# A hybrid Fourier/pooling encoder block on one core: xn is transposed by VectorE in squares of 32 instead of by TensorE, and the sums of the seven products of `w_out` are begun in PSUM from copies that ScalarE puts into the banks

## The reference, cut to what matters

```python
h = rmsnorm(x, norm1_g)
z = h @ w_in
ya = fourier_mix(z[..., :512]) ; yb = pool_mix(z[..., 512:])
x = x + concatenate([ya, yb]) @ w_out          # the stage of this change
h = rmsnorm(x, norm2_g)                        # its result is stored transposed
x = x + (silu(h @ w_gate) * (h @ w_up)) @ w_down
return rmsnorm(x, normf_g)
```

## Time and profile before

| | before |
|---|---|
| time, median of 3 runs (lowest to highest) | 2491.96 us (2491.36 to 2492.42) |
| profiled execution: its time, its span | 2491.23 us, 2489.4 us |
| TensorE, VectorE, ScalarE busy | 99%, 67%, 39% of the span |
| granted clock of TensorE | 1.00 in every stretch |
| pairs 2 to 11 of the output projection | 384 to 593 us, 20.86 us for each |

### The profile page before, as it was taken

The page is one execution under the profiler, slowest core; times in us unless marked ns, Lnnn a source line. Parts: engine busy times, 40 slices in busy tenths (PEclk is TensorE's granted clock), DMA queues, the critical chain, the costliest instruction groups (busy, mean ns, idle before and its releaser), DMA issues.

```text
span 2489.4 us, 32156 instructions
## 1 busy us (share of the span) xinstructions
PE 2474.7 (99%) x11141; PEld 2049.1 (82%) x11141; DVE 1676.6 (67%) x2600; ACT 965.2 (39%) x1830; POOL 166.9 (7%) x222
## 2 busy tenths in 40 slices
PE   9999999999999999999999999999999999999998
PEld 7888878887888888888888888888888888888887
DVE  5555788779767767877677687666774564455565
ACT  5534566667333333433333343333332232233333
POOL 2555400000000000000000000000000000000000
PEclk9999999999999999999999999999999999999999
DMA  6433767666423222532232432232346654354554
GB/s 184 115 85 99 223 221 254 238 238 260 157 80 116 97 103 110 195 113 110 80 126 101 155 146 96 110 110 89 118 186 217 242 200 168 119 196 149 195 189 148
DMA packets 154373, 381.99 MB, mean 153 GB/s; under 512 B 11992, under 2 KB 48184, under 8 KB 145076
## 3 DMA queue, kind: packets, MB, share of 16 engines
q1 hardware_dynamic: 145616, 350.81, 40.8%
q0 software_dynamic: 8240, 29.94, 3.2%
q10 hardware_dynamic: 432, 0.14, 0.0%
HBM read 254.22 MB, written 126.62 MB: 153 GB/s over the span
## 4 chain that ended last, share of the span: by engine, by line
PE 85%; DVE 2%; ACT 1%; issue 0%; DMA 0%; DVEq 0%
PE bank L351 28%; PE bank L353 28%; PE bank L352 28%; PE bank L2020 1%; ACT a_hi L2401 0%; DVE a_lo L2592 0%; DMA a_raw<-ha_scr 0%; PE bank L1373 0%; PE bank L1059 0%; DVE x L1818 0%; ACT h_out L1637 0%; DVE scratch L1033 0%; DVE zy_late L1044 0%; DVE uv_lo L1071 0%; ACT xn L1627 0%
## 5 line engine op out<-in xcount | busy, mean ns | idle before, releaser
L351 PE MATMUL bank<-a_hi,w_hi 128*128 128x512 f32 x1848 | 719.4, 389 | 2.0 <-DVE w_lo L2603 1.6
L352 PE MATMUL bank<-a_lo,w_hi 128*128 128x512 f32 x1848 | 718.9, 389 | 0.0
L353 PE MATMUL bank<-a_hi,w_lo 128*128 128x512 f32 x1848 | 718.9, 389 | 0.0
L351 PEld LDWEIGHTS bank<-a_hi,w_hi 128*128 128x128 f32 x1848 | 346.9, 188 | 75.6 <-DVE w_lo L2603 2.8
L353 PEld LDWEIGHTS bank<-a_hi,w_lo 128*128 128x128 f32 x1848 | 347.0, 188 | 72.0
L352 PEld LDWEIGHTS bank<-a_lo,w_hi 128*128 128x128 f32 x1848 | 347.0, 188 | 71.7
L351 PE MATMUL bank<-t_hi,s_hi 128*128 128x512 f32 x924 | 359.4, 389 | 0.0
L352 PE MATMUL bank<-t_lo,s_hi 128*128 128x512 f32 x924 | 359.4, 389 | 0.0
L353 PE MATMUL bank<-t_hi,s_lo 128*128 128x512 f32 x924 | 359.4, 389 | 0.0
L2414 ACT ACTIVATE w_hi<-t_raw 128x512 fp32r<-128x512 f32 x256 | 162.3, 634 | 462.4 <-PE bank L353 378.8
L2753 DVE TENSOR_TENSOR s_lo<-s_raw,s_hi 128x512 fp32r<-128x512 f32 x231 | 156.2, 687 | 230.7 <-ACT s_hi L2489 230.7
(11 more groups left out here) (277 smaller groups left out, 3163.1 us busy)
## 6 DMA issues: line engine op xcount, KB each, us to landing
s_scr<-sums_out SPq DMA_DIRECT2D x33, 1792.0 KB, 5.9
s_raw<-s_scr SPq DMA_DIRECT2D x42, 1024.0 KB, 5.0
w_raw<-in_w_gate SPq DMA_DIRECT2D x64, 512.0 KB, 3.5
w_raw<-in_w_up SPq DMA_DIRECT2D x64, 512.0 KB, 4.3
wd_staged<-in_w_down SPq DMA_DIRECT2D x121, 256.0 KB
a_raw<-ha_scr SPq DMA_DIRECT2D x21, 1024.0 KB, 5.0
s_raw<-s_scr SPq DMA_DIRECT2D x21, 768.0 KB, 4.4
x<-in_x SPq DMA_DIRECT2D x24, 512.0 KB, 4.9
```

The costliest lines, as they stand in the source:

```text
L351: pe.matmul(out, w_hi, m_hi, start=first, stop=False, **checks)
L352: pe.matmul(out, w_hi, m_lo, start=False, stop=False, **checks)
L353: return pe.matmul(out, w_lo, m_hi, start=False, stop=last, **checks)
```

## The change

On TensorE, the transposes go for 20 of the 24 tiles (tiles 0, 1, 22 and 23 keep them). VectorE turns xn in squares of 32x32 in their stead, four instructions of 128x512 for a pair (`turn_squares`). A square-wise transpose leaves the features spread differently over partitions, so that the gain is now a value of each partition and square: ScalarE multiplies `h_out` in place in 32 instructions of 2x32 columns for a pair (`gains`), where `stage_h` had 16 of 128. The rows reach their places in DRAM through the stores: `store_squares` has 8 + 4 stores of 32 partitions in packets of 512 bytes, 3584 of them for a pair. The token order inside a block changes, and the feed-forward matmuls read it back by a moving operand of 16 runs of 32 columns (`tokens_of`), where it was 4 runs of 128.

The sums of the seven products change too. ScalarE copies the first product (bank 0) into bank 1, TensorE adds the third product on top of it, ScalarE copies that sum into bank 3, and TensorE adds the fifth and the seventh on it. `u_sums` with its five VectorE additions becomes two (`add_held`). The two norms of a pair are one (`variance`, `inverse` over two columns), and so `scaled` of both tiles stands behind it. `combine` moves to the end of VectorE's pair.

```diff
-        def u_sums(n, k, par):
-            ...
+        def add_held(n, k, par, i):
+            tile, c, bank = ((1, 1, 2), (0, 1, 1))[i]
...
+            dve.tensor_tensor(at, o_ps[bank][:, :], at, ALU.add).then_inc(u_summed, 1)
...
+        def turn_squares(n, a, tile):
+            if (a, tile) == (0, 0):
+                dve.wait_ge(halves_out, halves_stored(n - 1))
+            if a == 0:
+                dve.wait_ge(xn_ready, n * 2 + (tile + 1))
+            half = xn[:, tile, a * HALF:(a + 1) * HALF].rearrange("p (k m f) -> p m k f", m=ROWS, f=SQUARE)
+            done = dve.transpose(h_out[:, tile, 4 * a:4 * a + 4, :].rearrange("p m (k t) -> p m k t", t=SQUARE), half)
...
+        def gains(n, a, first, last):
+            act.wait_ge(transposed, turned(n, a))
+            for b in range(first, last):
+                m, k = divmod(b, 4)
+                d = 4 * a + k
+                both = h_out[:, :, 4 * a + m, k * SQUARE:(k + 1) * SQUARE]
+                out = act.activation(both, both, ACT.Identity, scale=gain_squares[:, m, d:d + 1])
...
         def copy_product(n):
-            act.activation(U[:, :], o_ps[0][:, :], ACT.Copy).then_inc(p_copied, 1)
+            act.activation(o_ps[1][:, :], o_ps[0][:, :], ACT.Copy).then_inc(p_copied, 1)
+
+        def copy_sum(n):
+            act.wait_ge(pair_ready, product_of(n, 2))
+            act.activation(o_ps[3][:, :], o_ps[1][:, :], ACT.Copy).then_inc(p_copied, 1)
...
-        MORE = (False, False, False, True, False, True, True)
+        MORE = (False, False, True, True, True, True, True)
...
-            transposes(n * 2 - 2, slot)
             ready(S2, T2)
+            pe.wait_ge(p_copied, n * 2 - 3)
             seventh(S2)
-            transposes(n * 2 - 1, slot + 1)
...
+            pe.wait_ge(p_copied, n * 2 - 2)
             seventh(S3)
...
+        def store_squares(n):
+            sp.wait_ge(h_staged, staged(n))
+            for i in range(ROWS):
+                ... (2 stores of h_out rows i*32 to i*32+32)
+            sp.wait_ge(h_combined, n * 4 + 4)
+            for i in range(ROWS):
+                ... (1 store of h_sums)
...
+        def tokens_of(a, k):
+            return a[:, :, :].rearrange("p q (i k t) -> p (q i) k t", i=ROWS, t=SQUARE)[:, :, k, :]
```

More of the change, by code:

```diff
@@ L1559, in pair @@
             next_x(2 * n - 1, slot + 1, before + 1)
-            store_h(n - 1, 1 - par)
+            store_squares(n - 1)
         def load_a(s):
-            sp.dma_start(ahead.a_raw[s][:, :, :], ha_scr[A_ORDER[s], 0, :, :, :]).then_inc(ahead.a_loaded[s], DMA)
+            sp.dma_start(ahead.a_raw[s][:, :, :], ha_scr[0, A_ORDER[s], :, :, :]).then_inc(ahead.a_loaded[s], DMA)
         for n in range(2, LAST):
             if n == LAST - 1:
-                for par in range(2):
-                    sp.wait_ge(h_stored[par], 2 * 3 * DMA)
+                sp.wait_ge(halves_out, halves_stored(3))
+                sp.wait_ge(sums_out, sums_stored(3))
             pair(n)
@@ L1650, in scalar @@
         round_y(1)
-        act.wait_ge(ahead.gains_loaded, 2 * DMA)
+        act.wait_ge(ahead.gains_loaded, (2 + ROWS) * DMA)
         round_y(2)
@@ L1686, in pair @@
             round_v(after, k_after, 1 - par, A11)
-            scaled(n * 2 - 1, slot + 1)
-            stage_h(n * 2 - 2, slot, (h_stored[par], k * (3 * DMA)))
+            scaled(n, slot)
+            scaled(n, slot + 1)
             round_v(after, k_after, 1 - par, S1)
-            stage_h(n * 2 - 1, slot + 1)
-            for v in (S2, A12, S3):
-                round_v(after, k_after, 1 - par, v)
+            copy_sum(n)
+            gains(n - 1, 0, 0, 16)
+            round_v(after, k_after, 1 - par, S2)
+            gains(n - 1, 1, 0, 8)
+            round_v(after, k_after, 1 - par, A12)
+            gains(n - 1, 1, 8, 16)
+            round_v(after, k_after, 1 - par, S3)
             squares(n * 2, 2 * par, n * 4 + 3)
             round_v(after, k_after, 1 - par, S4)
-            root(n * 2, 2 * par)
         in_turn(act, pair)
-        round_v(LAST, NT // 4 - 1, 1, A22)
-        scaled(NT - 4, 0)
+        norms(LAST, NT // 4 - 1, 1)
+        scaled(LAST, 0)
+        scaled(LAST, 1)
         act.wait_ge(y_ready, split(LAST, A22))
         feed.round_a(0, 0)
[L1702 to L1707, removed]
+        copy_sum(LAST)
+        gains(LAST - 1, 0, 0, 16)
         feed.round_a(0, 1)
         feed.round_w(0, 0, 0, 0)
-        stage_h(NT - 3, 1)
+        gains(LAST - 1, 1, 0, 16)
         feed.round_w(0, 0, 0, 1)
@@ L1934, in vector @@
         rounds = NT // 4 - 1
-        c21(LAST - 1, 0)
-        for v in (A22, S3, S4):
-            rest_of_v(LAST, 1, v)
+        norms(LAST, 1)
         feed.rest_of_a(0, 0)
-        variance(NT - 3, 1)
-        inverse(NT - 3, 1)
-        u_sums(LAST, rounds, 1)
+        for a in range(2):
+            for tile in range(2):
+                turn_squares(LAST - 1, a, tile)
+        for i in range(2):
+            add_held(LAST, rounds, 1, i)
         feed.rest_of_a(0, 1)
@@ L2069, in tensor @@
         products(1)
-        transposes(0, 0, first=True)
+        transposes(0, 0)
         products(2)
-        transposes(1, 1, first=True)
+        transposes(1, 1)
         products(3)
```

236 lines of the change are left out of this document (125 added, 111 removed).

## The result

| | before | changed |
|---|---|---|
| time, median (lowest to highest) | 2491.66 us (2491.12 to 2492.42) | 2548.36 us (2547.77 to 2549.86) |
| ratio, 95% interval | | 1.0228 (1.0211 to 1.0246) |
| span of the profiled execution | 2489.4 us | 2545.8 us |

The change makes the kernel 57 us slower. 2496 was forecast, with a range to 2506. The page of the changed kernel looks much like the earlier trace rows: TensorE is still busy 99%.

A forecast was written before the change was run, and what follows sets the result against it. TensorE, 99% busy, bounds the kernel before; in changed pairs the VectorE and ScalarE ring binds at 20.3 us. 2491.2 − 5.0 + 8.6 = 2494.8, 2495.5 at the runs' median, half a us for waits: 2496, range 2485 to 2506.

The forecast's parts named there:

- Feed-forward operand: Gate and up matmuls: reading the moving operand in 16 runs of 32 columns costs nothing, as 4 runs match one.
- The bound above: Feed-forward operand: at most 1 ns for each of 12 more runs in 5544 matmuls, 66 us.
- 0.07: Chance that the operand costs TensorE something, or an unseen wait: over 2510 us, or 2560 us at the bound.
- TensorE, 1.78 us a pair: Output projection: two transpose groups removed from each pair save 1.78 us, leaving 84 matmuls in 19.04 us.
- g = 0.25: ScalarE's pace for one gain instruction of 64 columns in place: 0.25 us, bounds 0.17 and 0.30.
- The ring of 14.33 + 24g: VectorE and ScalarE hand-offs once a pair: 20.3 us at g = 0.25, over TensorE's 19.04; likeliest case, chance 0.40.
- The transposes, 4.04 us: VectorE's four square-wise transposes a pair: 1.01 us each, 4.04 in all; bounds 0.60 and 1.1 each.
- DMA, the second rival: Stores at the loads' rate bind pairs from the fourth on, 21.0 to 21.3 us each: 2501 to 2504, chance 0.22.
- 3.6 was my term: DMA queues, each pair: the stores in 512-byte packets take 8.95 us in place of 5.35.
- rows 8: Profile rows of loads in 512-byte packets at 205 GB/s, taken as the rate of the new stores.
- 5.0 saved by pair 11: Output projection, pairs 2 to 10: 182.7 us together against 187.7 before, 5.0 saved.
- 8.6 lost in pair 11 and the first tile: Hand-over to feed-forward: A22 waits for a late `c22`, VectorE's chain behind it stays; 53.0 us against 44.4.

The follow-up runs named there:

- e2: Kernel before, with only the moving operand of gate and up read in 16 runs of 32 columns, 128 columns apart: 2545.39 us, ratio 1.0210.
- e9: Kernel before, with only the moving operand of gate and up read in 32 runs of 16 columns, 64 columns apart: 2580.42 us.
- e1: Changed kernel, with the moving operand of gate and up read in 4 runs of 128 columns again: 2497.49 us, ratio 1.0018 to before.
- e6: Changed kernel with 4 runs of 128 in gate and up, and every second gain instruction left out: 2495.04 us, ratio 1.0009 to before.
- e7: Changed kernel with 4 runs of 128 in gate and up, half of the gains and stores in 2 KB packets: 2491.09 us, ratio 0.9994 to before.
- e5: Changed kernel with 4 runs of 128 in gate and up, its twelve stores a pair in 2 KB packets: 2492.71 us, ratio 1.0001 to before.

## Why the prediction was wrong

**The step that failed** is "Feed-forward operand. Its 16 runs of 32 columns cost nothing, I take it". It carries 54 of the 57 us. The argument was that 4 runs have the pace of 1, and it extrapolated from there to 16, over a distance in which the trace of before has no row. The bound above was worked out (1 ns a run, 66 us for all, close to the 54 measured), but given 0.07 together with everything unseen. With a bound that large on 5544 instructions of the engine that is 99% busy, and nothing but an extrapolation against it, it belonged in the range. What the runs showed in its place: 10.0 ns more for each of these matmuls, in the changed kernel and in e2 alike. The Trainium skill would have misled in the same way: Advanced Engine Details and Errata, SBUF Cachelines, gives full performance to accesses that hit the same line of 16 bytes. Inside runs of 128 bytes (e2) and 64 bytes (e9) they do, and the measurement disagrees.

**The rest** was forecast at 2496. It was measured at 2497.5 as e1, and the trace of the changed kernel gives about 2494. That this is so near is partly luck, since the terms err in both directions. They are:

- TensorE, 1.78 us a pair: right, the early pairs of e6 and e7 run at 19.04 to 19.08.
- g = 0.25: measured 0.24. The estimate from the Trainium skill (VectorE: DVE Perf Modes, the TRN2 errata) was 0.24 too, and the trace agrees. The ring of 14.33 + 24g is then 20.1, less 0.4 for a transpose that takes 0.61 and not 1.01: 19.7. Measured 19.8 to 19.9, in the early pairs, and e6 shows that it is this ring.
- The transposes, 4.04 us: mis-sized; four take 2.4, the lower bound.
- DMA, the second rival: its ring is there, but later and cheaper than I gave it, and made otherwise. Late pairs have 20.35 to 20.55 in the changed kernel, not 21.0 to 21.3. The queues are busy 17.3 us a pair and not 18.2: 2.6 more than before, of which e5 gives 1.3 to the small packets, where 3.6 was my term. The ring closes over SyncE's queue, in which the issue of twelve stores takes 7.1 us; I had put that at nothing. The Trainium skill's line rate from 512 bytes on (DMA: Bandwidth & Descriptors, Specifications) would make the 1.3 zero. Against e5 it is nearer to the stores than rows 8 were, but not right either.
- 5.0 saved by pair 11: measured 7.7. Half of the difference is the start, where pairs 2 and 3 take 19.0 and 20.1 and not 19.4 and 21.2, and half the seven pairs behind them, 140.8 us and not 142.1.
- 8.6 lost in pair 11 and the first tile: measured 10.1 (7.7 + 2.4). The place (`c22` ahead of A22, then VectorE's chain unchanged) was right, and so was most of the cause. I had ScalarE's gains end 19.4 us into pair 11 and `c22` 24.8; they end at 18.4 and 25.9. What I missed stands between them: the load of `a_raw`, issued 12.3 us into the pair and 5.6 before, holds `a_hi` 2.2 us longer than the gains do. It stands behind the twelve stores of a queue that is late, whose issue I had costed at nothing here as well. The clock's fall was not foreseen, but its cost is hidden.
- Chances: the 0.07 came true.

## What to carry to other kernels

Where a change alters how the busiest engine reads an operand, its price times the count of the instructions is the first term of the sum, and a shape outside what the trace shows is a bound and not a zero: run that one line alone (e2) before building what needs it. The transposes taken off TensorE were worth 17.8 us at most; the layout that they forced on it cost three times that, in another stage. Twelve stores in place of three take 7.1 us of the issuing queue in place of 1.6, and every load behind them comes later; look for who needs it, in the pair and in the stage that follows.

## What the runs showed of the hardware

- A float32 matmul of 512 moving columns, granted clock 1.00: runs of 128 and of 64 columns have the same spacing (0.227 us); 10 ns more at 32 (4%), whether they start 128 or 64 columns apart, 16 ns more at 16 (7%). With the short-run matmul one in three, 5.6 ns more on each.
- A VectorE transpose in squares of 32, 128x512 float32: 0.61 us, the pace of any VectorE operation of that size; in the first stage it is 1.01, and the reason for the difference wasn't looked for.
- ScalarE in place in SBUF, 64 columns: 0.24 us, about that of 128 columns from PSUM (0.25).
- TensorE idle for 6.8 us (changed kernel): granted clock 0.50 until 596.3, 6 us after its work began again. Idle for 2.2 us (e6): 0.43 us for each matmul from 536.95 on, and 0.23 again from 540.20. Waits of 1.2 us and less, once a pair, leave it at 1.00.
- The issue of small stores on SyncE's queue: twelve of 32 partitions (64 to 256 KB) take 7.1 us, and a load that waits for a store to land holds all behind it.
